# Retention chunks in a two-group decoder step: products of rounded parts in place of float32 products

## The reference, cut to what matters

```
# per head, chunks of C = 128 tokens; D is the lower triangle of decays
scores = einsum('ihd,jhd->hij', q, k) * D
intra  = einsum('hij,jhe->ihe', scores, v)
cross  = einsum('ihd,hde->ihe', q * q_decay, S)
S      = S * c_decay + einsum('jhd,jhe->hde', k * k_decay, v)
o      = intra + cross
o      = o * rsqrt(mean(o * o) + eps) * silu(g)
```

## Time and profile before

| what | value |
| --- | --- |
| median of 3 runs | 2937.08 us (2935.84 to 2937.14) |
| the profiled execution's own time | 2937.58 us |
| its span, first to last instruction | 2935.8 us |
| PE busy | 2878.7 us, 98% |
| DVE, ACT, POOL busy | 1195.6, 696.2, 145.9 us |
| mean granted clock of PE | 0.996 |
| the four chunk stages | at 117 to 172, 365 to 421, 615 to 671, 866 to 922 us |

### The profile page before, as it was taken

How to read it: one execution, slowest core, us unless ns; L and a number is a source line. 1 busy time by engine, 2 the same in 40 slices (tenths; PEclk the granted TensorE clock), 3 DMA queues, 4 the chain that set the end, 5 groups by cost and what they waited for, 6 DMA issues and landing times.

```text
span 2935.8 us, 42461 instructions
## 1 busy us (share of the span) xinstructions
PE 2878.7 (98%) x17576; PEld 2717.4 (93%) x17576; DVE 1195.6 (41%) x1468; ACT 696.2 (24%) x1206; POOL 145.9 (5%) x114
## 2 busy tenths in 40 slices
PE   8999999999999999999999999998999999999999
PEld 8789969969987999999999999975899999999999
DVE  6343443444344633233332345456543333333333
ACT  3231131123123322111221132135322221122111
POOL 0000000000000200000000012134220000000000
PEclk9999999999999999999999999999999999999999
DMA  3221132122113111111111112220011111111112
GB/s 131 94 87 60 39 135 67 44 100 76 60 58 115 41 51 41 46 47 45 46 43 46 43 43 82 68 84 15 22 44 47 47 43 43 49 43 46 44 46 77
DMA packets 91092, 173.21 MB, mean 59 GB/s; under 512 B 9792, under 2 KB 15168, under 8 KB 90304
## 3 DMA queue, kind: packets, MB, share of 16 engines
q1 hardware_dynamic: 89056, 166.10, 17.9%
q10 hardware_dynamic: 1920, 5.41, 0.8%
HBM read 142.54 MB, written 25.56 MB: 57 GB/s over the span
## 4 chain that ended last, share of the span: by engine, by line
PE 92%; DVE 4%; ACT 2%; issue 1%; DMA 0%; POOL 0%; SPq 0%; ACTq 0%; DVEq 0%
PE ps L1274 81%; PE ps L1415 2%; PE ps L1421 1%; DVE wlo L835 1%; PE ps L1672 1%; PE ps L1314 1%; PE ps L1410 1%; PE ps L1645 1%; DVE s L945 1%; PE ps L1656 1%; PE ps L1398 1%; PE ps L1383 1%; ACT e_a L753 1%; ACT o_tok L623 1%; PE ps L1442 0%
## 5 line engine op out<-in xcount | busy, mean ns | idle before, releaser
L1274 PE MATMUL ps<-hhi,whi 128*128 128x352 f32 x3168 | 689.4, 326 | 11.7 <-DVE hlo L843 8.5
L1274 PE MATMUL ps<-hlo,whi 128*128 128x352 f32 x3168 | 686.7, 325 | 0.0
L1274 PE MATMUL ps<-hhi,wlo 128*128 128x352 f32 x3168 | 681.7, 323 | 0.0
L1274 PEld LDWEIGHTS ps<-hhi,whi 128*128 128x128 f32 x3168 | 537.6, 189 | 13.9 <-DVE hlo L843 8.5
L1274 PEld LDWEIGHTS ps<-hhi,wlo 128*128 128x128 f32 x3168 | 542.7, 189 | 0.0
L1274 PEld LDWEIGHTS ps<-hlo,whi 128*128 128x128 f32 x3168 | 540.6, 188 | 0.0
L835 DVE TENSOR_TENSOR wlo<-wraw,whi 128x512 fp32r<-128x512 f32 x424 | 333.2, 793 | 471.2 <-ACT whi L569 471.1
L569 ACT CAST whi<-wraw 128x512 fp32r<-128x512 f32 x424 | 261.0, 619 | 1105.6 <-PE ps L1274 1099.7
L873 DVE TENSOR_TENSOR x<-ps,x 128x1056 f32<-128x1056 f32 x168 | 211.0, 1256 | 541.4 <-PE ps L1274 541.3
L1274 PE MATMUL ps<-ahi,whi 128*128 128x352 f32 x1920 | 416.2, 325 | 2.1 <-DVE x L873 2.1
L1274 PE MATMUL ps<-alo,whi 128*128 128x352 f32 x1920 | 414.6, 324 | 0.0
(11 more groups left out here) (163 smaller groups left out, 1658.2 us busy)
## 6 DMA issues: line engine op xcount, KB each, us to landing
wraw<-in_weights SPq DMA_DIRECT2D x424, 256.0 KB, 2.6
s<-in_state_in SPq DMA_DIRECT2D x32, 512.0 KB, 3.7
out_state_s<-s SPq DMA_DIRECT2D x32, 512.0 KB, 2.8
zr<-z_a ACTq DMA_DIRECT2D x40, 132.0 KB, 2.4
x<-in_xT SPq DMA_DIRECT2D x8, 528.0 KB, 8.5
rope_tab<-in_tables SPq DMA_DIRECT2D x4, 1056.0 KB, 4.9
out_yT<-x SPq DMA_DIRECT2D x8, 528.0 KB, 2.7
out_state_p<-s_ret SPq DMA_DIRECT2D x4, 512.0 KB, 2.8
```

What stands on the lines that cost most here:

```text
L1274: mm = pe.matmul(ps[:, 3 * (m % 2) + t, 0:TB], a[:, slot, w], b[:, s * KG + k, t * TB:(t + 1) * TB], start=(first and j == 0), stop=(last ...
```

## The change

1. k by v and scores by v use three float32r products of rounded parts. New buffers hold high and low parts of v, k and the scores; DVE makes the low ones (`keep_v_low` for v, more steps in `decay_keys`).
2. The copies of sample keys and values lie by groups, so that each sequence pair's terms lie in 32 rows. `sample_states` forms one half of the features of two sequences at a time from 32 rows each; `select` is done twice a head instead of eight times; `update_samples` comes ahead of `inverse_rms`. State stores wait for a pair.
3. `turn_v` is called after the first slab of products 5, 6 and 7.
4. The outputs are kept in the place of q and k (`o_t = qk`), the gate works in the place of v (`gate_q`), `v_lo` lies where the outputs were; the load of the rope table waits for the gates of the head before.

```diff
             def store_state(h, b):
-                sp.wait_ge(s0_upd, h * NB + (b + 1))
+                sp.wait_ge(s0_upd, h * NB + (b // 2 * 2 + 2))
...
                     slabs(quad, 0, 4)
-                    sp.wait_ge(ot_kept, h * (CH + 1))
+                    sp.wait_ge(a_lo, h * 4)
...
+                ins = dve.tensor_tensor(sc_t[:, c % 2, 0:rows], ps[:, score_bank(c), DK:DK + rows],
+                                        hmask[:, P:P + NS] if c == CH else hmask[:, 0:P], ALU.mult)
+                if c == CH:
+                    ins.then_inc(sc_kept, 1)
+                else:
+                    ins.then_inc(dve_seq, 1)
+                    seq[0] += 1
 
             def decay_keys(h, c):
                 n = h * (CH + 1) + (1 if c == CH else c + 2)
                 dve.wait_ge(kt_done, n)
                 if 2 <= c < CH:
                     dve.wait_ge(st_done, h * CH + (c - 1))
-                dve.tensor_scalar(k_tok[:, c % 2, :], ps[:, score_bank(c), 0:DK], kdec, None, ALU.mult
-                                  ).then_inc(kt_kept, 1)
-
-            def select(h, b):
-
-                dve.tensor_scalar(k_sel[:, b % 2, :], f32(k_smp[:, :]), cst[:, C_BM + b:C_BM + b + 1], None, ALU.mult
-                                  ).then_inc(sel_ready, 1)
+                keys = ps[:, score_bank(c), 0:DK]
+                if c == CH:
+                    dve.tensor_scalar(k_tok[:, :], keys, kdec, None, ALU.mult).then_inc(kt_kept, 1)
+                    return
+                dve.tensor_scalar(k_hi[:, c % 2, :], keys, kdec, None, ALU.mult).then_inc(dve_seq, 1)
+                seq[0] += 1
+                dve.wait_ge(dve_seq, h * N_SEQ + seq[0] - 1)
+                dve.tensor_copy(sc_hi[:, c % 2, :], sc_t[:, c % 2, :]).then_inc(dve_seq, 1)
+                seq[0] += 1
+                dve.wait_ge(dve_seq, h * N_SEQ + seq[0] - 1)
+                dve.scalar_tensor_tensor(out=k_lo[:, c % 2, :], in0=keys, scalar=kdec, in1=f32(k_hi[:, c % 2, :]),
+                                         op0=ALU.mult, op1=ALU.subtract).then_inc(kt_kept, 1)
+                dve.wait_ge(dve_seq, h * N_SEQ + seq[0])
+                dve.tensor_tensor(sc_lo[:, c % 2, :], sc_t[:, c % 2, :], f32(sc_hi[:, c % 2, :]), ALU.subtract
+                                  ).then_inc(sc_kept, 1)
+
+            def keep_v_low(h, e):
+
+                for half in range(2):
+                    high = v_hi[:, 4 * half:4 * half + 4, e * P:(e + 1) * P]
+                    dve.wait_ge(v_kept, h * 9 + (2 * e + half + 1))
+                    dve.tensor_tensor(v_lo[:, 4 * half:4 * half + 4, e * P:(e + 1) * P],
+                                      ps[:, 6 + half, :].rearrange("p (c f) -> p c f", c=4), f32(high), ALU.subtract
+                                      ).then_inc(v_low, 1)
+
+            def select(h):
+
+                for half in range(2):
+                    dve.tensor_scalar(k_sel[:, half, :], f32(k_smp[:, :]), cst[:, C_BM + half:C_BM + half + 1], None,
+                                      ALU.mult).then_inc(sel_ready, 1)
 
             def spread_queries(h):
 
...
-            def update_sample(h, b):
-                dve.wait_ge(sts_done, h * NB + (b + 1))
-                dve.scalar_tensor_tensor(out=s0[:, b % S0_RING, :, :], in0=s0[:, b % S0_RING, :, :],
+            def update_samples(h, c):
+
+                slot = c // 2 * 2 % S0_RING
+                part = s0[:, slot:slot + 2, c % 2, :]
+                dve.wait_ge(sts_done, h * NB + (c + 1))
+                dve.scalar_tensor_tensor(out=part, in0=part,
                                          scalar=hc[:, H_CDS:H_CDS + 1], in1=ps[:, 0:2, :],
                                          op0=ALU.mult, op1=ALU.add).then_inc(s0_upd, 1)
 
-            def stack(h, whole, parts, low):
+            def stack(h, whole, parts):
 
                 link(h, dve.tensor_copy(parts, whole))
-                for k, rows in enumerate(low):
-                    ins = dve.tensor_tensor(parts[rows, :], whole[rows, :], f32(parts[rows, :]), ALU.subtract)
-                    if k + 1 < len(low):
-                        ins.then_inc(dve_seq, 1)
-                        seq[0] += 1
-                return ins
+                return dve.scalar_tensor_tensor(out=parts, in0=f32(parts), scalar=cst[:, C_NK:C_NK + 1], in1=whole,
+                                                op0=ALU.mult, op1=ALU.add)
 
...
                 for m in range(4, 8):
                     split(quad, 2 * m, 2 * m + 2)
                     if m == 4:
                         dve.wait_ge(dve_seq, h * N_SEQ + seq[0])
-                        dve.tensor_copy(k4[:, :, :, :], qk[:, 2:4, SEQ:TOK].unsqueeze(2).to_broadcast([P, 2, 4, NS])
-                                        ).then_inc(four_ready, 1)
+                        for j in range(2):
+                            dve.tensor_copy(k4[:, j, :, :, :], by_term(qk[:, 2 + j, SEQ:TOK])).then_inc(four_ready, 1)
                         spread_queries(h)
                     elif m == 5:
                         mask_scores(h, CH)
                         decay_keys(h, CH)
                         dve.wait_ge(sc_kept, h * (CH + 1) + 1)
-                        stack(h, sc_t[:, 0, 0:NS], sc_smp[:, :], odd).then_inc(sel_ready, 1)
+                        stack(h, sc_t[:, 0, 0:NS], sc_smp[:, :]).then_inc(sel_ready, 1)
                         dve.wait_ge(kt_kept, h * (CH + 1) + 1)
-                        link(h, stack(h, k_tok[:, 0, :], k_smp[:, :], odd))
+                        link(h, stack(h, k_tok[:, :], k_smp[:, :]))
+                        select(h)
+                    if m > 5:
+                        keep_v_low(h, m - 6)
                     read_normed(m, n + (2 * m + 2), tmp[:, m - 4, :])
                     dve.wait_ge(mt_free, mt + (m + 1))
-                    dve.tensor_copy(v4[:, m - 4, :, :], tmp[:, m - 4, SEQ:TOK].unsqueeze(1).to_broadcast([P, 4, NS])
-                                    ).then_inc(four_ready, 1)
+                    dve.tensor_copy(v4[:, m - 4, :, :, :], by_term(tmp[:, m - 4, SEQ:TOK])).then_inc(four_ready, 1)
+                keep_v_low(h, 2)
+                keep_v_low(h, 3)
                 mask_scores(h, 0)
                 decay_keys(h, 0)
                 dve.wait_ge(v_kept, h * 9 + 9)
-                low = slice(64, 128)
-                dve.tensor_tensor(v_smp[low, :], ps[low, 4, :], f32(v_smp[low, :]), ALU.subtract).then_inc(vs_ready, 1)
-                select(h, 0)
+                dve.scalar_tensor_tensor(out=v_smp[:, :], in0=f32(v_smp[:, :]), scalar=cst[:, C_NV:C_NV + 1],
+                                         in1=ps[:, 4, :], op0=ALU.mult, op1=ALU.add).then_inc(vs_ready, 1)
                 for c in range(CH):
                     update_state(h, c)
                     if c + 1 < CH:
                         mask_scores(h, c + 1)
                         decay_keys(h, c + 1)
-                        select(h, c + 1)
+                    update_samples(h, c)
                     inverse_rms(h, c)
-                    update_sample(h, c)
                 inverse_rms(h, CH)
...
                     if e:
-                        pe.wait_ge(v_kept, h * 9 + (2 * e + half - 1))
+                        pe.wait_ge(v_low, h * 8 + (2 * e + half - 1))
                     elif half:
                         pe.wait_ge(kt_kept, h * (CH + 1) + 1)
                         pe.wait_ge(sc_kept, h * (CH + 1) + 1)
...
                 pe.wait_ge(kt_kept, i + 2)
                 if c:
                     pe.wait_ge(s0_upd, h * NB + c)
+                if c == 0:
+                    pe.wait_ge(v_low, (h + 1) * 8)
                 for j in range(2):
-                    mm = pe.matmul(ps[:, j, :], k_tok[:, c % 2, j * P:(j + 1) * P], v_tok[:, c, :],
-                                   start=True, stop=True)
+                    feats = slice(j * P, (j + 1) * P)
+                    pe.matmul(ps[:, j, :], k_hi[:, c % 2, feats], v_hi[:, c, :], start=True, stop=False)
+                    pe.matmul(ps[:, j, :], k_hi[:, c % 2, feats], v_lo[:, c, :], start=False, stop=False)
+                    mm = pe.matmul(ps[:, j, :], k_lo[:, c % 2, feats], v_hi[:, c, :], start=False, stop=True)
                 mm.then_inc(st_done, 1)
                 if c + 1 < CH:
                     keys_and_scores(h, c + 1)
                 pe.wait_ge(sc_kept, i + 2)
-                pe.matmul(ps[:, bank, :], sc_t[:, c % 2, :], v_tok[:, c, :], start=(c == 0), stop=True
+                pe.matmul(ps[:, bank, :], sc_hi[:, c % 2, :], v_hi[:, c, :], start=(c == 0), stop=False)
+                pe.matmul(ps[:, bank, :], sc_hi[:, c % 2, :], v_lo[:, c, :], start=False, stop=False)
+                pe.matmul(ps[:, bank, :], sc_lo[:, c % 2, :], v_hi[:, c, :], start=False, stop=True
                           ).then_inc(o_done, 1)
...
-            def sample_state(h, b):
-
-                pe.wait_ge(sel_ready, h * (1 + NB) + (1 + (b + 1)))
```

(50 more changed lines are left out.)

35 lines of the change are left out of this document (20 added, 15 removed).

## The result

The changed kernel takes 2959.9 us (2957.0 to 2966.8, four runs) beside 2936.5 of the kernel before on the same chips: ratio 1.0084, 95% interval 1.0069 to 1.0099. Forecast were 2958 us and a range of 2940 to 2974. The profiled execution took 2960.0 us, span 2958.2.

A forecast was written before the change was run, and what follows sets the result against it. TensorE was taken to bound the kernel (92% of the chain of waits). Per head −6.8 + 0.2 + 6.7 + 0.9 + 2.0 = +3.0, four heads +12, clock +9: 2937.6 + 12 + 9 − 0.5 = 2958 us, range 2940 to 2974.

The forecast's parts named there:

- What bounds, and where it counts: Whole kernel: TensorE is 92% of the chain of waits, so its own instructions and standstills count, four times for four heads.
- Chunk stage, gain 6.8: Chunk 0 to chunk 7 of each head: 49.42 us become 42.65, with even chunks at 6.50 and odd at 5.55.
- Low-part prices taken from neighbours: DVE's new steps, priced from similar rows: high scores 0.40, low keys 0.20, low scores 0.40, each keep_v_low half 0.69 us.
- Stalls in the products, 6.7 a head: turn_v inside products 5, 6 and 7: PE waits for DVE, 1.76 + 2 × 2.49 us; 5.7 with 0.35 a half.
- Third turn 0.9: Turn inside product 7: formerly under DVE's read of the last tile before, now on the path, costing 0.9 us a head.
- start 2.0: From the last V product to the first chunk: 6.73 us, before 4.73, so 2.0 us more per head.
- Terms set at nothing: Paired state stores and later loads, rope table's wait, stack, select, copies by term, outputs over q and k: no cost.
- Clock, six falls at 1.5: New stalls and chunk starts, three places a head: half of twelve bring a clock fall at 1.5 us, +9 us.
- the turns do stall: Against the faster rival, turns inside products without stalls: 6.7 us a head goes, 2922 us, chance 0.10.
- the products were 0.23, not 0.285: Against the dearer rival in the chunks: nine products at 0.285 us and row tiles one after the other, 2981 us, chance 0.10.
- the low parts not at half the price: Against the balance rival: keep_v_low halves at 0.35 us and no clock falls, +0.8 us a head, 2940 us, chance 0.07.
- The clock's fall at every place: Rival at the new stalls and chunk starts: all twelve places fall, 20 us in place of 9, 2969 us, chance 0.12.

The follow-up runs named there:

- e2: Changed kernel, turns left inside the products, with DVE's sample scores and keys and keep_v_low put ahead of the second slab's split: 2930.7 us, ratio 0.9988.
- e1: Changed kernel with turn_v called after the second slab of products 5 to 7 again, all else kept: 2924.2 us, ratio 0.9959.
- e3: Kernel before the change with only the turns moved inside the products: 2947.5 us, ratio 1.0046.
- e4: Changed kernel with update_samples behind inverse_rms again, turns still inside the products: 2972.6 us, ratio 1.0119.
- e5: Changed kernel with plain float32 products for k by v and scores by v, no low parts, turns after the second slab: 2927.8 us, ratio 0.9971.

## Why the prediction was right, step by step

- **What bounds, and where it counts:** held. The time went into PE's standing still at places named by line and engine.
- **Chunk stage, gain 6.8:** 49.42 became 42.61 in head 1, as worked out (42.65). Even and odd chunks were set at 6.50 and 5.55. The ends of q by state (L1454) lie 5.55 and 6.60 apart. (L1462 starts 5.81 and 6.34 apart, but its start is recorded while the product still waits.) The agreement of the whole to 0.04 is in part luck: the even chunks take 0.10 more than set, three times, and chunk 0, which was set at 6.50, takes 6.14. The 0.23 for a product whose weights are loaded ahead and the 0.20 for a change of shape were right.
- **Low-part prices taken from neighbours:** high scores 0.22, low keys 0.48, low scores 0.28, a half of `keep_v_low` 0.68. The row on half the partitions (0.69) was the right one; partitions don't count there.
- **Stalls in the products, 6.7 a head:** gaps of 2.66, 3.37 and 3.37 give 1.7 + 2.4 + 2.4 = 6.5. e2 and e1 show the cause, e3 the share of the calls alone. (The 5.7 that the prediction gives for halves at 0.35 is a slip: by its own steps each of the two later stalls would shrink by 2 x 0.34, which gives 5.4. The forecast doesn't use it.)
- **Third turn 0.9, start 2.0:** e3 shows the first, in the last turn's wait; head 1's 6.75 for 4.73 the second.
- **Terms set at nothing:** held. In PE's list of waits there is none for a transfer.
- **Clock, six falls at 1.5:** seven, in heads 0, 2 and 3, all at or right behind a new stall or the start of a chunk stage. From the last product of tile 4 (331.04) to the gate (431.54), head 1, without a fall, took 100.50 us for 97.61, so +2.9 where the sum has +3.0; the others took 6.5, 5.1 and 6.8 more. The 9.7 us above 2.9 each, over seven falls, are 1.4 a fall. The price was read from rows; the number was not. Half of twelve was a guess, and that seven came in this profile is luck. The largest uncertainty of the sum was well placed: the four runs of the changed kernel differ by 10 us, with the mean clock from 0.993 in the fastest to 0.990 in the slowest.
- **Rivals:** the turns do stall; the products were 0.23, not 0.285; the low parts not at half the price. The clock's fall at every place did not come: head 1 has none in 6.75 us of transposes and waits. The Trainium skill ("TensorE: Matmul & The Clock Gate", Part 4) says that transposes don't count as busy in the same way, which speaks for one there. This trace agrees in heads 0, 2 and 3 and disagrees in head 1; what decides between the heads stays open.

Two sizes in the experiments were off, mostly about chunk 0 and the tail, which I had treated as like the other chunks: e4's price was set 3 us too low, e5's gain 5 us too high by the gate (8 by the medians). An average chunk was multiplied by eight where the first and the last hang on other things.

## What to carry to other kernels

A call placed between two halves of a product meets whatever its partner engine has queued behind the release of the first half. Before moving one, write down what stands ahead of the needed instruction in the other engine's program and what releases that; a split that waits for a ring slot is such a gate. If two engines hand work to and fro, put the instruction that the other engine waits for ahead of the refill (as in e2), or place the call half a product later (as in e1). And when a start is shortened, look at once at the transfer that was hidden there.

## What the runs showed of the hardware

- Two products with 32 rows in different row groups and different banks run side by side also in float32r: L1505's pair lasts 0.50 us. A change of the array's shape costs 0.20 there, and 0.14 and 0.19 around L1442 of the kernel before. "TensorEngine Tiling (Array Packing)", Key Properties, in the Trainium skill says that changing the mode drains the array; the traces show no drain as such, but a pause at each change, of these 0.14 to 0.20 us.
- Three float32r products of 512 columns cost 0.70 us where one float32 product costs 0.86.
- A fall of the granted clock, in head 2 of the changed kernel (columns as in rows 2), comes after a stall inside a product: PE is busy for 3.23 of 5.27 us at 1.00 (2.4 GHz), the turn's wait among them, and then runs the slab's products at 0.50 (1.2 GHz).

```profile
604.50:609.77 5.27, 3.23 (x22) 2.77 (x21) 1.89 (x3) 1.48 (x3) 0.00 (x0) 1.00 0.00 0
609.78:613.19 3.41, 3.41 (x13) 3.41 (x13) 0.00 (x0) 0.30 (x1) 0.00 (x0) 0.50 0.02 5
```

- At the start of the chunks the clock fell where the start was long. It lasts 6.7 us or more in four kernels (after, e1, e2, e4), and there 0.50 was granted for a stretch of the start or of chunk 0 in 13 of 16 heads. It lasts 4.6 to 6.1 us in the other six, and there in none of 24. Why it spares three of the sixteen is not shown.
- The part from the gate of head 3 to the end, at which none of the edits is aimed, took 2011.8 to 2017.6 us in the ten profiles. So up to 6 us of a comparison of single executions are not the edit's.
